# x's log decays made with features on partitions, summed by VectorE's prefix scans

## The chip, the cores and the metric

The kernel runs on one core of one Trainium2 chip. The metric is the device time of one execution in microseconds; lower is better. The engines are named as the profile names them: PE (TensorE's matmuls, with PEld for its weight loads), DVE (VectorE), ACT (ScalarE), POOL (GpSimd) and SP (SyncE, which here issues most of the loads).

## The reference

Two transformer blocks over 256 tokens of width 2048. The change lies in the second one, in its gated linear attention over x (4 heads, key width 128 each, so 512 key features; the 256 tokens are 2 chunks of 128; one gate runs forward, one backward):

```python
la = log_sigmoid(d @ wd2 + bd) / 16          # log decay, one per token and key feature, for each way
# per chunk and way:
b = cumsum(la, over tokens)                  # running sums
b_last = b[-1]                               # whole chunk
scores[i, j] = sum_d q[i,d] k[j,d] exp(b[i,d] - b[j,d])      (j <= i)
o = scores @ v + (q * exp(b)) @ s
s = exp(b_last) * s + (k * exp(b_last - b)).T @ v            # the state that the next chunk takes
```

The same is done for the 256 context tokens before, which only leave their state `s`. The rest of the block (the projections, a spatial gating, the output product and a feed-forward part) is matrix products with `w_in_2`, `w_out_2` and so on.

## The kernel before

Every large product is made from chunks of weights: SP loads a 128 x 2 x 512 piece of weights into one of 4 slots of `ring`, DVE forms from it the sums that a seven-product (Strassen-like) scheme needs (`step(n)`: lines 1098 and 1099 are `step_first`, 1107 and 1109 are `step_last`), and PE multiplies (`chunk`, line 636: 14 products of 128x256, 28 passes in the trace, since an f32 product is two passes). `step` for chunk m makes the sums of chunk m+2, into one of 3 slots of `sums`. When a group of four chunks is done, ACT copies its first product (`first_keep`, line 2008) and DVE gathers the seven into the result (lines 1131 to 1141).

Each engine has its own program in a fixed, hand-written order. The order of what is done beside the chunks of the projection of x is a table, `MIX_BESIDE`: to (group, chunk) belongs a list of items, and each engine, when it has done its own part for that chunk, goes through the items and does what it has to do for each. The items that matter here, for the groups 1 and 2 (the keys k were group 0, the queries q are group 1):

- `la`: PE makes the log decays' raw values (line 879), ACT takes Abs, Exp, Ln of them, DVE ends them (`la_end`, lines 1540 and 1542).
- `k_turn`, `k_place`, `q_turn`, `q_place`: a 128x1024 tile is transposed in two steps, DVE's 32x32 block transposes (line 1190), then 16 copies of blocks by ACT (`place_blocks`, line 2043 or 2045).
- `cum`: PE makes the running sums of la as products with a triangular matrix (line 942), ACT copies them from PSUM to `b_t`, which has features on partitions (line 2377).
- `rem`: PE makes the remaining decays (the sums of la behind each token) with two other triangular matrices (line 949), ACT takes their Exp into `qe` (line 2395).
- `kdec`: DVE multiplies `qe` with the keys (line 1687); `upd` later has PE multiply this with the values.
- `level`: the scores are made in 8 levels of halved blocks. For each, DVE takes differences of `b_t` (line 1608), ACT takes their Exp (line 2345, two instructions), DVE and POOL multiply them with queries and keys (lines 1623 and 2720), and PE, behind the chunk to which the item belongs, multiplies the two (line 977). In PE's program this waits for DVE's and POOL's results:

```python
elif item[0] == "level":
    pe.wait_ge(s["lv_q"], lv + 1)
    pe.wait_ge(s["lv_k"], lv + 1)
```

On ACT the two Exp of a level come ahead of the other items of the same chunk. On DVE a level's differences come ahead of `step_first`, its product comes behind that, then `step_last`, then the other items of the chunk.

## Time and profile before

| | |
|---|---|
| median of 3 runs | 2707.28 us (2707.27 to 2708.39) |
| the profiled execution's own time | 2707.41 us |
| its span, from first to last instruction | 2705.6 us |
| PE busy | 2693.7 us, 100% of the span |
| DVE busy | 2108.5 us, 78% |
| ACT busy | 861.7 us, 32% |
| POOL busy | 315.0 us, 12% |
| DMA | 571.88 MB, mean 211 GB/s |

The span is that of one execution, recorded on the chip. The 1.8 us between the span and the execution's own time lie ahead of the first and behind the last instruction. Matmuls overlap, so that PE busy means that it had work, not that it was at its peak.

### The profile page before, as it was taken

Reading aid. Unit: us, or ns where it says so; the run is one execution under the profiler, and the core shown is the slowest. Engines: PE = TensorE matmul, PEld = TensorE weight load, DVE = VectorE, ACT = ScalarE, POOL = GpSimd, SP = SyncE. Lnnn points to the kernel's source line nnn. Section 1 sums busy time; section 2 is a strip of 40 time slices with the busy share of each in tenths; the row PEclk is TensorE's granted clock in tenths of the full one; section 3 lists DMA queues with packets and bytes.
Section 4 is the critical chain, followed back from the end, with each engine's and each line's share of the span. In section 5 each row is a group of like instructions: output and inputs, shape, how many; then the busy total and the mean of one; then the engine's idle time right before and its main releaser. Section 6 shows DMA issues by size and latency. Waiting matters only on the chain.

```text
span 2705.6 us, 27692 instructions
## 1 busy us (share of the span) xinstructions
PE 2693.7 (100%) x9684; PEld 1725.2 (64%) x9684; DVE 2108.5 (78%) x3066; ACT 861.7 (32%) x1986; POOL 315.0 (12%) x500
## 2 busy tenths in 40 slices
PE   9999999999999999999999999999999999999998
PEld 8888888886444444444447888888444444444487
DVE  7988887987999999998887677886866667664444
ACT  2455655332453534530036442331321211111000
POOL 2112231000101111010101012100010010100000
PEclk9999999999999999999999999999999999999999
DMA  8888777677666667668775655554576676656554
GB/s 279 246 264 255 250 236 232 206 235 237 218 221 219 214 218 221 221 233 275 259 273 167 172 171 141 148 186 157 172 223 219 214 221 217 187 164 202 174 175 132
DMA packets 277660, 571.88 MB, mean 211 GB/s; under 512 B 26056, under 2 KB 27420, under 8 KB 277008
## 3 DMA queue, kind: packets, MB, share of 16 engines
q1 hardware_dynamic: 244384, 460.05, 54.3%
q0 software_dynamic: 32704, 109.73, 12.5%
q8 instruction: 76, 1.25, 0.2%
q14 instruction: 64, 0.52, 0.1%
q10 hardware_dynamic: 432, 0.34, 0.0%
HBM read 565.91 MB, written 4.11 MB: 211 GB/s over the span
## 4 chain that ended last, share of the span: by engine, by line
PE 77%; issue 20%; DVE 1%; POOL 1%; POOLq 1%; DMA 0%; DVEq 0%; ACT 0%; ACTq 0%
PE PS L651 44%; PE PS L636 30%; PE PS L665 0%; DMA ring<-in_w_branch_a 0%; PE PS L924 0%; PE PS L774 0%; PE PS L800 0%; PE PS L977 0%; PE PS L722 0%; POOLq L2583 0%; POOL mem L2584 0%; PE PS L779 0%; POOLq L2581 0%; POOL small L2711 0%; PE PS L696 0%
## 5 line engine op out<-in xcount | busy, mean ns | idle before, releaser
L1098 DVE TENSOR_TENSOR sums<-ring 128x512 f32<-128x512 f32 x429 | 299.8, 699 | 411.6 <-PE PS L651 260.3
L651 PE MATMUL PS<-sums,mem 128*128 128x512 f32 x1100 | 561.5, 592 | 0.0
L636 PE MATMUL PS<-ring,mem 128*128 128x256 f32 x1936 | 543.8, 380 | 0.1
L636 PE MATMUL PS<-sums,mem 128*128 128x256 f32 x1792 | 533.0, 379 | 0.0
L651 PE MATMUL PS<-ring,act_t 128*128 128x512 f32 x1056 | 511.0, 592 | 1.4 <-issue 1.0
L651 PE MATMUL PS<-ring,mem 128*128 128x512 f32 x880 | 438.6, 592 | 0.0
L636 PEld LDWEIGHTS PS<-ring,mem 128*128 128x128 f32 x1936 | 365.9, 190 | 52.1 <-issue 2.1
L651 PEld LDWEIGHTS PS<-sums,mem 128*128 128x128 f32 x1100 | 209.0, 190 | 263.1 <-issue 262.8
L636 PEld LDWEIGHTS PS<-sums,mem 128*128 128x128 f32 x1792 | 340.5, 190 | 46.3
L651 PEld LDWEIGHTS PS<-ring,act_t 128*128 128x128 f32 x1056 | 200.1, 190 | 251.2 <-issue 246.6
L2008 ACT COPY first_q<-PS 128x256 f32<-128x256 f32 (+1 forms) x73 | 32.5, 445 | 1010.5 <-PE PS L651 669.0
L2043 ACT COPY mem<-mem 32x256 f32<-32x256 f32 (+1 forms) x784 | 313.4, 400 | 123.2 <-DVE mem L1935 84.8
L1109 DVE TENSOR_TENSOR sums<-sums,ring 128x512 f32<-128x512 f32 x429 | 302.1, 704 | 14.9
L1231 DVE SCALAR_TENSOR_TENSOR mem<-mem,small 128x1024 f32<-128x1024 f32 x240 | 302.0, 1279 | 8.6 <-DMA mem<-in_w_mod 8.5
L1107 DVE TENSOR_TENSOR sums<-sums,ring 128x512 f32<-128x512 f32 x429 | 302.0, 704 | 0.0
L1099 DVE TENSOR_TENSOR ring<-ring 128x512 f32<-128x512 f32 x431 | 300.8, 698 | 0.0
L651 PEld LDWEIGHTS PS<-ring,mem 128*128 128x128 f32 x880 | 167.0, 190 | 209.6 <-issue 208.3
L2595 POOL DMA_DIRECT2D mem<-in_w_mod x192 | 103.8, 541 | 1438.9 <-DVE mem L1231 1241.3
L636 PE MATMUL PS<-ring,act_t 128*128 128x256 f32 x976 | 265.1, 379 | 0.0
L636 PEld LDWEIGHTS PS<-ring,act_t 128*128 128x128 f32 x976 | 184.7, 190 | 26.8 <-issue 1.4
L651 PE MATMUL PS<-sums,act_t 128*128 128x512 f32 x352 | 179.8, 592 | 0.1
L651 PEld LDWEIGHTS PS<-sums,act_t 128*128 128x128 f32 x352 | 66.8, 190 | 84.6 <-issue 84.6
(305 smaller groups left out, 1935.3 us busy)
## 6 DMA issues: line engine op xcount, KB each, us to landing
ring<-in_w_in SPq DMA_DIRECT2D x240, 512.0 KB, 4.1
mem<-in_w_mod POOLq DMA_DIRECT2D x192, 512.0 KB, 4.7
ring<-in_w_up SPq DMA_DIRECT2D x176, 512.0 KB, 4.4
ring<-in_w_ffn_in SPq DMA_DIRECT2D x176, 512.0 KB, 4.6
ring<-in_w_down SPq DMA_DIRECT2D x88, 512.0 KB, 4.9
ring<-in_w_ffn_out SPq DMA_DIRECT2D x88, 512.0 KB, 3.8
ring<-in_w_out SPq DMA_DIRECT2D x64, 512.0 KB, 3.8
ring<-in_w_branch_a SPq DMA_DIRECT2D x16, 512.0 KB, 4.3
```

The lines of the kernel that those rows point to most:

```text
L636: mm = pe.matmul(product(g, j), of(j, 2 * (c if part is None else part) + q), weights(j, n, q), start=lead and opens, stop=tail, skip_grou ...
L651: mm = pe.matmul(product(g, j), of(j, c), weight[j], start=lead, stop=tail, skip_group_check=True)
L1098: ve.tensor_tensor(one, b11, b12, ADD).then_inc(s["sums_ready"], 1)
L1099: ve.tensor_tensor(b12, b22, b12, ADD)
L1107: ve.tensor_tensor(two, one, b22, ADD).then_inc(s["sums_ready"], 1)
L1109: ve.tensor_tensor(three, two, b21, ADD).then_inc(s["sums_ready"], 1)
L1231: op = ve.scalar_tensor_tensor(acc[which], wm[:, h % 2, :], col, acc[which], MUL, ADD)
L2008: act.copy(to, product(g, Q1)).then_inc(s["first_kept"], 1)
L2043: act.copy(to, from_[:, :, 0:tiles, b_, :])
L2595: pool.dma_start(wm[:, h % 2], w_mod[:, kt, col:col + 2 * CN]).then_inc(wm_loaded[h % 2], 16)
```

## The change

PE now makes x's raw log decays transposed: the weights `wd2` are the stationary operand and the projected tokens `d_t` the moving one, so that the result has features on partitions and tokens along the row. This takes 16 products of 128 columns where there were 4 of 512 (both on 32 rows of the array each). The running sums are made by four prefix scans of DVE (`tensor_tensor_scan`) straight into `b_t`; a tile `go_on` that is 1 except for a 0 at each head's first token restarts the sum. PE's `cum` and `rem` products are gone. The remaining decays are Exp(whole - b) on ACT, eight instructions of 128x128, each with its own bias column; the result has features on partitions, so DVE multiplies it with the transposed keys `k_t`, transposes it in blocks, and ACT places the blocks with 16 copies into `k_tok` (`kdec_place`). POOL's next two loads of `w_mod` wait for `la_done` where they waited for `rem_done`. The table names in TURN0 only shift by one.

```diff
-                      (1, 3): [("gather", 1), ("cum",)], (2, 0): [("q_turn",), ("q_place",)], (2, 1): [("rem", 0), ("rem", 1)],
-                      (2, 2): [("level", 0, 0), ("kdec", 0), ("kdec", 1)],
+                      (1, 3): [("gather", 1)], (2, 0): [("q_turn",), ("q_place",), ("cum",)], (2, 1): [("rem",)],
+                      (2, 2): [("level", 0, 0), ("kdec",), ("kdec_place",)],
...
 (PE)        def log_decay(m):
                 pe.wait_ge(s["d_placed"], m + 1)
-                for h in range(2):
-                    for r in range(2):
-                        rows = slice(64 * h + 32 * r, 64 * h + 32 * r + 32)
+                quarters = [(h, r, slice(64 * h + 32 * r, 64 * h + 32 * r + 32)) for h in range(2) for r in range(2)]
+                if m == 0:
+                    for h, r, rows in quarters:
                         mm = pe.matmul(PS[:, 4 + 2 * h + r, :], d_t[rows, h * P:(h + 1) * P], wd2[rows, :], start=True,
                                        stop=True)
+                else:
+                    for hd in range(GH):
+                        for h, r, rows in quarters:
+                            mm = pe.matmul(PS[:, 4 + 2 * h + r, hd * P:(hd + 1) * P], wd2[rows, hd * P:(hd + 1) * P],
+                                           d_t[rows, h * P:(h + 1) * P], start=True, stop=True)
...
-                    elif item[0] == "cum":
-                        pe.wait_ge(s["la_ready"], 2)
-                        for n in range(2):
-                            for r in range(2):
-                                for hd in range(GH):
-                                    mm = pe.matmul(PS[:, 4 + 2 * n + r, hd * P:(hd + 1) * P],
-                                                   la[:, n, r, hd * P:(hd + 1) * P], tri[:, r, :], start=True,
-                                                   stop=True)
-                        mm.then_inc(s["cum_done"], 1)
-                    elif item[0] == "rem":
-                        r = item[1]
-                        pe.wait_ge(s["cum_kept"], 1)
-                        mm = pe.matmul(PS[:, 6 + r, :], tri[:, 2 + r, :], la[:, r, r, :], start=True, stop=True)
-                        mm.then_inc(s["rem_done"], 1)
                     elif item[0] == "upd":
                         r = item[1]
-                        pe.wait_ge(s["kdec_ready"], 3 + r)
+                        pe.wait_ge(s["kdec_placed"], 1)
...
 (DVE)
+                    elif item[0] == "cum":
+                        ve.wait_ge(s["state_done"], 2)
+                        ve.wait_ge(s["la_ready"], 2)
+                        ve.memset(go_on, 1.0)
+                        ve.drain()
+                        ve.memset(go_on[:, 0:CN:P], 0.0)
+                        ve.drain()
+                        for n in range(2):
+                            for r in range(2):
+                                way = slice(None, None, 1 - 2 * r)
+                                op = ve.tensor_tensor_scan(b_t[:, n, r, way], go_on, la[:, n, r, way], 0.0, MUL, ADD)
+                        op.then_inc(s["cum_kept"], 1)
...
                     elif item[0] == "kdec":
-                        r = item[1]
-                        ve.wait_ge(s["rem_exp"], 2 + r)
-                        ve.tensor_tensor(qe[:, r, :], qe[:, r, :], k_tok[:, r, :], ALU.mult)\
-                            .then_inc(s["kdec_ready"], 1)
-                        if r == 1:
-                            ve.memset(s_t[:], 0.0)
+                        ve.wait_ge(s["rem_exp"], 2)
+                        for r in range(2):
+                            part = qe[:, r, :].rearrange("p (h i) -> p h i", i=P)
+                            ve.tensor_tensor(part, part, k_t[:, :, r * P:(r + 1) * P], ALU.mult)
+                        flat = qe.rearrange("p r f -> p (r f)")
+                        turn_in_blocks(flat, flat)
+                        ve.memset(s_t[:], 0.0)
...
 (ACT)
-                    elif item[0] == "cum":
-                        act.wait_ge(s["cum_done"], 1)
-                        act.copy(b_t.rearrange("p a b c -> p (a b) c"), PS[:, 4:8, :]).then_inc(s["cum_kept"], 1)
...
                     elif item[0] == "rem":
-                        r = item[1]
-                        act.wait_ge(s["rem_done"], 2 + r)
-                        act.activation(qe[:, r, :], PS[:, 6 + r, :], ACT.Exp).then_inc(s["rem_exp"], 1)
+                        act.wait_ge(s["cum_kept"], 1)
+                        for r in range(2):
+                            edge = HD - 1 if r == 0 else 0
+                            for hd in range(GH):
+                                whole = b_t[:, r, r, hd * P + edge:hd * P + edge + 1]
+                                op = act.activation(qe[:, r, hd * P:(hd + 1) * P], b_t[:, r, r, hd * P:(hd + 1) * P],
+                                                    ACT.Exp, bias=whole, scale=-1.0)
+                        op.then_inc(s["rem_exp"], 1)
+                    elif item[0] == "kdec_place":
+                        turned(act, "kdec", 0)
+                        for a_ in range(4):
+                            for b_ in range(4):
+                                from_ = qe[32 * a_:32 * a_ + 32].rearrange("p r (h b c) -> p r h b c", b=4, c=32)
+                                to = k_tok[32 * b_:32 * b_ + 32].rearrange("p r (h d) -> p r h d", d=P)
+                                act.copy(to[:, :, :, 32 * a_:32 * a_ + 32], from_[:, :, :, b_, :])
+                        act.drain().then_inc(s["kdec_placed"], 1)
...
 (POOL)
-            pool.wait_ge(s["rem_done"], 3)
+            pool.wait_ge(s["la_done"], 2)
             mod_loads(2)
```

What stands in a row on ACT between the queries' placing (L2045) and the Exp of the levels 0 and 1 (L2345, the shapes 4x64 and 8x32), before:

```order
L2008 COPY first_q<-PS 128x256
L2377 COPY mem<-PS 128x2048
L2045 ACTIVATE mem<-mem 32x2x4x32 x16
L2395 ACT_TABLE_LOAD
L2395 ACTIVATE mem<-PS 128x512 x2
L2345 ACTIVATE mem<-mem 128x2x4x64 x2
L2345 ACTIVATE mem<-mem 128x2x8x32 x2
L2008 COPY first_q<-PS 128x256
```

The same place of ACT's program in the changed kernel, whose line numbers are 4 higher there:

```order
L2012 COPY first_q<-PS 128x256
L2049 ACTIVATE mem<-mem 32x2x4x32 x16
L2399 ACT_TABLE_LOAD
L2399 ACTIVATE mem<-mem 128x128 x8
L2349 ACTIVATE mem<-mem 128x2x4x64 x2
L2408 COPY mem<-mem 32x8x32 x16
L2349 ACTIVATE mem<-mem 128x2x8x32 x2
L2012 COPY first_q<-PS 128x256
```

The copy of the running sums is gone, the two Exp of 128x512 are eight of 128x128, and the 16 placing copies (L2408) stand between the Exp of level 0 and those of level 1.

On DVE, from the sums behind the queries' block transposes (L1190) to the differences of level 1 (the second L1608), before:

```order
L1190 STREAM_TRANSPOSE mem<-mem 128x1024
L1098 TENSOR_TENSOR sums<-ring 128x512
L1099 TENSOR_TENSOR ring<-ring 128x2x256
L1107 TENSOR_TENSOR sums<-sums,ring 128x512
L1109 TENSOR_TENSOR sums<-sums,ring 128x512
L1608 TENSOR_TENSOR mem<-mem 128x512 x2
...
L1687 TENSOR_TENSOR mem<-mem 128x512 x2
L1690 MEMSET mem 128x512
L1608 TENSOR_TENSOR mem<-mem 128x512 x2
```

And in the changed kernel, where these lines are 8 lower (4 higher behind the new item):

```order
L1182 STREAM_TRANSPOSE mem<-mem 128x1024
L1667 MEMSET mem 128x512
L1669 MEMSET mem 128x4
L1674 SCALAR_TENSOR_TENSOR mem<-mem 128x512 x4
L1090 TENSOR_TENSOR sums<-ring 128x512
...
L1691 TENSOR_TENSOR mem<-mem 128x512 x2
L1182 STREAM_TRANSPOSE mem<-mem 128x1024
L1694 MEMSET mem 128x512
L1600 TENSOR_TENSOR mem<-mem 128x512 x2
```

The four scans (listed as SCALAR_TENSOR_TENSOR) and two fills stand behind the queries' transposes, and another block transpose stands behind the two kdec products. On PE the 16 products of L942 and the two of L949 are gone.

## Rows read from the trace of the kernel before

**Rows 1.** The page: busy time of the engines, and the chain that ended last.

```profile
PE 2693.7 (100%) x9684; PEld 1725.2 (64%) x9684; DVE 2108.5 (78%) x3066; ACT 861.7 (32%) x1986; POOL 315.0 (12%) x500
...
PE 77%; issue 20%; DVE 1%; POOL 1%; POOLq 1%; DMA 0%; DVEq 0%; ACT 0%; ACTq 0%
```

**Rows 2.** The chain in order of time: start us, us, what.

```profile
1573.42 3.57 PE PS L942 x32
1576.99 12.09 PE PS L636 x56
1589.08 1.72 PE PS L949 x4
1590.80 6.04 PE PS L636 x28
1596.84 0.62 PE PS L977 x16
1597.45 6.24 PE PS L636 x28
1603.69 0.39 PE PS L977 x32
```

**Rows 3.** Timeline of PE: start us, us, engine, line, op, tiles, shapes, count.

```profile
1539.37 1.93 PE L862 MATMUL PS<-mem 128*32 128x256 f32 x32
...
1553.95 1.14 PE L879 MATMUL PS<-mem 32*128 32x512 f32 x8
```

**Rows 4.** Timeline of ACT, from the queries' placing to level 1.

```profile
1578.92 6.79 ACT L2045 ACTIVATE mem<-mem 32x256 f32<-32x256 f32 x16
1585.84 1.28 ACT L2395 ACT_TABLE_LOAD   x1
...
1591.45 1.15 ACT L2345 ACTIVATE mem<-mem 128x512 f32<-128x512 f32 x2
1598.57 1.15 ACT L2345 ACTIVATE mem<-mem 128x512 f32<-128x512 f32 x2 [5.97 <-DVE mem L1608]
```

**Rows 5.** Timeline of DVE, the same stretch.

```profile
1577.27 1.25 DVE L1190 STREAM_TRANSPOSE mem<-mem 128x1024 f32<-128x1024 f32 x1
1583.14 0.69 DVE L1098 TENSOR_TENSOR sums<-ring 128x512 f32<-128x512 f32 x1 [4.63 <-PE PS L636]
...
1592.73 1.36 DVE L1623 TENSOR_TENSOR mem<-mem 128x256 f32<-128x256 f32 x2 [2.26 <-ACT mem L2345]
...
1595.34 1.28 DVE L1687 TENSOR_TENSOR mem<-mem 128x512 f32<-128x512 f32 x2
1596.68 0.48 DVE L1690 MEMSET mem<- 128x512 f32 x1
...
1599.75 1.72 DVE L1623 TENSOR_TENSOR mem<-mem 128x256 f32<-128x256 f32 x2
```

**Rows 6.** Timeline of POOL, the keys of level 1.

```profile
1599.28 1.92 POOL L2720 TENSOR_TENSOR mem<-mem 128x256 f32<-128x256 f32 x2 [5.46 <-ACT mem L2345]
```

**Rows 7.** Timeline of ACT: a placing behind its transpose, and small activations with two column operands.

```profile
1534.18 6.61 ACT L2401 COPY act_t<-act_t 32x256 f32<-32x256 f32 x16 [5.78 <-DVE act_t L1678]
...
1899.98 0.81 ACT L2467 ACTIVATE act_t<-PS,small 128x128 f32<-128x128 f32 x2 [1.79 <-PE PS L1033]
```

**Rows 8.** The page's costliest groups: busy us, mean ns, idle before.

```profile
L1231 DVE SCALAR_TENSOR_TENSOR mem<-mem,small 128x1024 f32<-128x1024 f32 x240 | 302.0, 1279 | 8.6 <-DMA mem<-in_w_mod 8.5
```

**Rows 9.** Timeline of PE at the two ends of the span.

```profile
1.42 3.36 PE L722 MATMUL PS<-ones 128*128 128x128 f32 x14 [1.42 <-POOLq L2602]
4.57 1.06 PE L696 MATMUL PS<-ident,x_tok 128*128 128x128 f32 x4
...
8.02 0.60 PE L696 MATMUL PS<-ident,x_tok 128*128 128x128 f32 x4
...
2696.78 1.03 PE L602 MATMUL PS<-act_t,mem 128*128 128x256 f32 x4
```

**Rows 10.** Windows: engines' busy us (count), granted PE clock, DMA share, GB/s.

```profile
2700.00:2701.00 1.00, 0.00 (x0) 0.00 (x0) 1.00 (x1) 0.00 (x0) 0.00 (x0) 0.64 0.00 0
```

More of the change, by code:

```diff
@@ L257, in build @@
         la, b_t = cut(3072, 2, 2, CN), cut(0, 2, 2, CN)
-        e_buf, qe = cut(5120, 2, CN), cut(6144, 2, CN)
+        e_buf, qe, go_on = cut(5120, 2, CN), cut(6144, 2, CN), cut(6144, CN)
         mix2_tmp, mix2_junk = [cut(7168 + 1024 * n, 2, CN) for n in range(3)], cut(7168, D)
@@ L301, in build @@
             "attn_done", "attn_kept", "bias_loaded", "bias_used", "ws_stored", "ws_spread", "c_ready",
-            "consts_loaded", "ctx_loaded", "cum_done", "cum_kept", "d_copied", "d_done", "d_kept", "d_placed", "d_summed",
+            "consts_loaded", "ctx_loaded", "cum_kept", "d_copied", "d_done", "d_kept", "d_placed", "d_summed",
             "decay_ready", "down_added", "exps_done", "gain_loaded", "ident_loaded", "forms_ab", "forms_ctx", "forms_ffn",
             "forms_ffn2", "forms_h", "forms_h2", "forms_hx", "forms_m", "forms_mix", "forms_w2", "den_ready", "x_first", "w_first", "sums_first", "gates_squashed",
-            "g_opened", "gate_loaded", "gate_ready", "gate_stored", "hidden_done", "job_acc", "half_done", "kdec_ready", "kt_kept", "la_done", "la_exp", "la_ready",
+            "g_opened", "gate_loaded", "gate_ready", "gate_stored", "hidden_done", "job_acc", "half_done", "kdec_placed", "kdec_ready", "kt_kept", "la_done", "la_exp", "la_ready",
             "levels_loaded", "lv_diff", "lv_done", "lv_exp_k", "lv_exp_q", "lv_k", "lv_q", "lv_taken", "masks_loaded", "max_ready",
@@ L394, in build @@
         TURN0 = {"heads": 0, "probs": 7, "merged": 15, "ffn": 19, "up": 23, "ctx": 45, "mix2": 49, "ws": 53, "k": 54, "q": 55,
-                 "y0": 56, "u0": 57, "y1": 58, "u1": 59, "ffn2": 58, "up2": 62}
+                 "kdec": 56, "y0": 57, "u0": 58, "y1": 59, "u1": 60, "ffn2": 59,
+                 "up2": 63}
         PLACE0 = {"heads": 0, "probs": 7, "merged": 15, "ffn": 19, "ctx": 23, "mix2": 27, "ffn2": 29}
@@ L936, in _ @@
                         log_decay(1)
-                    elif item[0] == "cum":
-                        pe.wait_ge(s["la_ready"], 2)
-                        for n in range(2):
-                            for r in range(2):
-                                for hd in range(GH):
-                                    mm = pe.matmul(PS[:, 4 + 2 * n + r, hd * P:(hd + 1) * P],
-                                                   la[:, n, r, hd * P:(hd + 1) * P], tri[:, r, :], start=True,
-                                                   stop=True)
-                        mm.then_inc(s["cum_done"], 1)
-                    elif item[0] == "rem":
-                        r = item[1]
-                        pe.wait_ge(s["cum_kept"], 1)
-                        mm = pe.matmul(PS[:, 6 + r, :], tri[:, 2 + r, :], la[:, r, r, :], start=True, stop=True)
-                        mm.then_inc(s["rem_done"], 1)
                     elif item[0] == "upd":
                         r = item[1]
-                        pe.wait_ge(s["kdec_ready"], 3 + r)
+                        pe.wait_ge(s["kdec_placed"], 1)
                         kept_all(pe, G0["mix"] + VV_GROUP + 1)
                         if r == 0:
-                            pe.wait_ge(s["rem_exp"], 3)
+                            pe.wait_ge(s["cum_kept"], 1)
                         else:
@@ L960, in _ @@
                             mm = pe.matmul(PS[:, 6 + hd // 2, (hd % 2) * T:(hd % 2) * T + T],
-                                           qe[:, r, hd * P:(hd + 1) * P], vv[:, r, hd * T:(hd + 1) * T],
+                                           k_tok[:, r, hd * P:(hd + 1) * P], vv[:, r, hd * T:(hd + 1) * T],
                                            start=True, stop=True)
@@ L1616, in level_close @@
                 if lv == 0:
-                    ve.wait_ge(s["rem_done"], 3)
                     ve.wait_ge(s["q_kept"], 1)
```

## The prediction

> **What bounds the kernel now.** I read the page first: PE has work for all of the span, and 77% of the chain that ended last is PE's matmuls, with nearly all the rest as PE's own issue [rows 1]. So what is taken off PE comes off the time one for one, and a new wait of PE is added one for one. DVE is busy for 78% and ACT for 32%; their work is free only as long as PE never stands for it. So the second view is the chain in order of time around the change [rows 2]: three chunks of 6.04 us, with the running sums (3.57 us) and the remaining decays (1.72 us) between them, then level 0, one chunk, level 1, back to back. There is no wait in it. The third views are the timelines of ACT and DVE beside it [rows 4 to 6], to see how early the results arrive that PE asks for. For level 1, PE comes at 1603.69; DVE's product for it ended at 1599.75 + 1.72 = 1601.47 and POOL's at 1601.20. That is 2.2 us of slack, and the change touches exactly the engines that fill it.
>
> **The change, part by part.** The sum is made against the profiled execution, 2707.41 us (median of the runs 2707.28, so 0.1 us apart).
>
> PE, removed: L942 3.57 us and L949 1.72 us, together -5.29 us [rows 2].
>
> PE, changed: the four 32-row products of 512 columns (8 passes, from 1553.95 to the next row at 1555.02, 1.07 us) become 16 of 128 columns (32 passes). They stream the same columns. The old ones plainly ran four beside each other: 8 passes of 512 columns one behind the other would take 8 x 0.43 = 3.4 us (0.43 being a quarter of L949's 1.72 us for 4 passes). If the new ones do so too, the nearest row is L862, 32 passes of 256 columns on quarters of the array in 1.86 us (1539.37 to the next row at 1541.23) [rows 3]; half the columns gives 0.93 us at the least. If none runs beside another, it is L942's price, 3.57 us. I take 1.2 us, near the lower end, since the order in the code still goes round the four quarters: +0.13 us, with ends at -0.14 and +2.5.
>
> DVE, added behind the queries' transpose, which ends at 1578.52: a fill of 128x512 (0.48 us), a tiny one, two drains (0.2 us together with it) and four scans. The trace shows no scan. By half of the 128x1024 row of the same listed operation, 1.28 us, one takes 0.64 us [rows 8]; as the upper end I take that whole row. So they end between 1581.8 and 1584.3. The cover is DVE's idle time of 4.63 us before 1583.14 [rows 5] and then the two chunks by which `step` runs ahead of PE. ACT asks for `b_t` at 1586.8 (below); DVE must still make one chunk's sums (four rows from 1583.14 on, 2.6 us) and two differences (1.3 us) before 1589.4. So the scans cost nothing up to (1589.4 - 3.9 - 1579.2) / 4 = 1.57 us each, and 4 us per us beyond that.
>
> The Trainium skill ("DVE: opcode table, instruction layouts, handler registers and perf-mode slots", section 6, Datapath and trigger behaviour) says that the built-in scan feeds its result back and runs at half throughput. No row here shows one; by that rule a scan would be about 1.2 us, still inside the cover, where by the row's price it is 0.64, and the sum is the same by both. It brings the limit nearer, though, and speaks for the last rival below.
>
> ACT, up to level 0: the copy of the running sums (between the gather's `first_keep` and 1578.92) is gone, so the queries' placing starts as the transpose ends, at 1578.56 (a placing starts some 0.04 us behind it, as L2401 does behind its own) instead of 1578.92. It takes 6.79 us, then 0.13 us and the table load of 1.28 us [rows 4]: 1586.76. Eight Exp of 128x128 with a bias column follow. Nearest is L2467, the same size with two column operands: two take 0.81 at 0.45 each, so one each 0.36 us, and eight take 2.97 [rows 7]. The other end is a quarter of half of the 1.15 us that two of 128x512 take, 1.15 us for eight. I take 2.6, near the row of the same size: 1589.4. From the start of the level's Exp to the end of DVE's product it was 1594.09 - 1591.45 = 2.64 us [rows 4, 5], so level 0 is ready at 1592.05. PE, after 12.09 + 6.04 us of chunks from 1573.42, asks for it at 1591.55. **First wait: 0.5 us** where there was none.
>
> The Trainium skill ("ScalarE: Activation LUTs", section What ACT_TABLE_LOAD costs) puts an activation with one column operand at 280 ns + 0.833 ns an element, with 93 ns of overlap between neighbours. That is 0.29 us for each of 128 columns and 2.4 for eight, and an estimate of the whole sum 0.2 us below mine.
>
> ACT, level 1: this is the step on which the prediction rests. In ACT's program the 16 copies of `kdec_place` stand between the Exp of level 0 and those of level 1. They need DVE's transpose of the kdec product, and that stands behind level 0's product and `step_last`. From DVE's level-0 product to its kdec products it was 1595.34 - 1592.73 = 2.61 us, and 1.34 us to the row behind them [rows 5]. With level 0's Exp at 1589.4, DVE's product starts 1.28 later at 1590.7, kdec at 1593.3, the transpose at 1594.65, ending at 1595.9 (1.25 as L1190). ACT's 16 copies take 6.61 us [rows 7] and a drain 0.1: 1602.65. Only then do level 1's Exp run; before, from their start at 1598.57 DVE's product took until 1601.47, 2.90 us [rows 4, 5], and POOL's until 1601.20, 2.63 us [rows 4, 6]. Level 1 is ready at 1605.55. PE, from 1592.1 on, does level 0 (0.62) and a chunk (6.24) and asks at 1598.95. **Second wait: 6.6 us.** Queued behind it on PE is all that follows; DVE's `step_last` and gather stand behind its product of level 1, ACT's `first_keep` behind the Exp. PE's next level comes two chunks (12 us) later, which I take as enough for DVE to catch up.
>
> So PE starts level 1 at 1605.6 instead of 1603.69: +1.9 us, and +2.05 with the log decays. As a ledger: -5.29 + 0.13 + 0.5 + 6.65 = +2.0.
>
> The clock: at the start of the span PE, having done nothing, runs 14 passes of 128 columns in 3.36 us, 0.24 us each, where 32 such take 3.57 us in mid-kernel, 0.11 each; four transposes take 1.06 us at 4.57 and 0.60 at 8.02 [rows 2, 9]. So it ran at the lower level (1.2 GHz) from 1.42 until about 7.1. At the end, PE's last row ends at 2697.8, and in the window from 2700 to 2701 the granted clock is 0.64, on its way to half [rows 9, 10]. So it falls some 2.5 us behind the last matmul. A wait of 6.6 us is longer than that. If PE then needs the 5.7 us that it needed at the start, it does 2.85 us' less work than at 2.4 GHz: **+2.85 us**. The end of this term towards nothing is a clock that stays or that rises at once.
>
> DVE, ACT and DMA elsewhere: nothing. POOL's two loads of `w_mod` (512 KB each) go out 36 us earlier, at about 1555, beside SP's ring loads. DVE then stands for ACT's Abs, Exp and Ln anyway. DVE's extra transpose and the strided kdec operand are in the chain above.
>
> Sum: -5.29 + 0.13 + 0.5 + 6.6 + 2.85 = +4.8 to 4.9, so 2707.4 + 4.9 = **2712.3 us**. What a measurement of this kernel can tell from no change is about 0.2%, 5.4 us: this forecast lies just inside it.
>
> **The rivals.**
> 1. As summed, with both waits and the lower clock: 2712.3. Its own range: the eight Exp move level 1 by -1.45 to +0.4, the time at the lower clock may be half or a fifth more of that at the start (-1.4 to +0.6), the copies by 0.5 each way: 2709.8 to 2714. Chance 0.68.
> 2. The waits come, the clock does not fall (or is back at once): 2707.4 + 2.05 = 2709.5 us. Against it stands the fall 2.5 us behind the last matmul [rows 9, 10]. Chance 0.10.
> 3. Not slower: the placing is hidden and PE keeps the whole saving, -5.16, so 2702.3. One thing would do it: ACT's chain from the queries' transpose to level 1 being 7.1 us shorter than I make it (1605.55 against 1598.4), from which on nothing is lost; it is no slower from 2.05 us shorter on, if the clock holds in the 4.6 us of waiting that are left. For it speaks only that the price of the eight Exp is not in the trace; against it, 6.61 us of copies and 6.79 of placing are rows. Chance 0.08.
> 4. More than summed: the 32-row products no longer run beside each other (+2.4, 2714.7), or scans above 1.57 us each (at 2 us, +1.7, 2714.0), or DVE, which comes out of level 1 later against PE than before, makes PE wait once more at the next levels (of 1 to 3 us). Chance 0.14.
>
> **How the numbers follow.** The predicted time is that of the first. From 2709.0 to 2715.3 the range takes in the first, the second and most of the fourth, and leaves out the third (0.08) and the fourth's far part. Slower by over 0.2% means above 2712.7: the fourth nearly whole (0.13) and some 0.4 of the first (0.27), together 0.40. Faster by over 0.2%, below 2701.9, is a third of the third case: 0.03. Within: 0.57.
>
> **What would show it.** In the changed kernel: ACT's 16 copies between the Exp of levels 0 and 1, starting about 1596 and ending about 1602.6; PE idle before level 1 for 6 to 7 us and before level 0 for less than 1, with DVE's or POOL's level product as releaser; the granted clock below 1 in a window behind it, and passes of 256 columns at twice 0.216 us for some 5 us; four scans of 0.6 to 1.3 us ending before ACT's table load; the 32-row products in 1.0 to 1.3 us. It is wrong if PE shows no wait before level 1, or if waits of DVE's or PE's turn up elsewhere of the same size.

## The result: 4.4 us slower, and the profile after

The changed kernel takes 2712.16 us, the median of 20 runs (2710.95 to 2713.22); the kernel before, beside it, 2707.72 us (2706.71 to 2708.39). The ratio is 1.0016, 95% interval 1.0010 to 1.0022. PE lost the 18 products of the running sums and the remaining decays, and the kernel became 4.4 us slower, 0.16%. That is less than the 0.2% of the prediction's bound, but the interval leaves out 1, so the slowdown is told from none. The profiled execution took 2712.94 us, its span 2711.1 us, so 5.5 us more than before.

The page of the changed kernel, with the lines that answer to [rows 1]:

```profile
PE 2691.7 (99%) x9672; PEld 1723.3 (64%) x9672; DVE 2115.2 (78%) x3073; ACT 867.3 (32%) x2007; POOL 313.2 (12%) x500
...
PE 76%; issue 20%; DVE 2%; ACT 1%; POOL 1%; POOLq 1%; DMA 0%; DVEq 0%; ACTq 0%
```

PE has 2 us less work, though the clock stretched some of it, and its share of the chain is a point lower; DVE and ACT have come into the chain. Which line they came in by is told by the view of PE's waits, changed kernel (line, releaser: us in total, times, longest):

```profile
PE PS L969 <- DVE mem L1614: 7.2, 3, 6.2
...
PE PS L637 <- DVE mem L1123: 0.4, 1, 0.4
```

L969 is the level's product on PE (before L977) and L1614 DVE's product for it (before L1623). Before there was no such wait in this stretch. ACT's timeline of the changed kernel, to be held against [rows 4]:

```profile
1578.32 6.80 ACT L2049 ACTIVATE mem<-mem 32x256 f32<-32x256 f32 x16 [7.31 <-DVE mem L1182]
1585.25 1.28 ACT L2399 ACT_TABLE_LOAD   x1
1586.55 2.45 ACT L2399 ACTIVATE mem<-mem 128x128 f32<-128x128 f32 x8
1588.90 1.13 ACT L2349 ACTIVATE mem<-mem 128x512 f32<-128x512 f32 x2
1595.42 6.61 ACT L2408 COPY mem<-mem 32x256 f32<-32x256 f32 x16 [5.39 <-DVE mem L1182]
1602.13 1.15 ACT L2349 ACTIVATE mem<-mem 128x512 f32<-128x512 f32 x2
```

The 16 copies (L2408) take ACT from 1595.42 to 1602.03, and only then do level 1's Exp run, 3.6 us later than before. DVE in the same stretch, to be held against [rows 5]:

```profile
1577.04 1.25 DVE L1182 STREAM_TRANSPOSE mem<-mem 128x1024 f32<-128x1024 f32 x1
1578.35 0.48 DVE L1667 MEMSET mem<- 128x512 f32 x1
1579.08 4.57 DVE L1674 TENSOR_TENSOR_SCAN mem<-mem 128x512 f32<-128x512 f32 x4
...
1590.13 1.40 DVE L1614 TENSOR_TENSOR mem<-mem 128x256 f32<-128x256 f32 x2 [1.56 <-ACT mem L2349]
...
1592.78 1.29 DVE L1691 TENSOR_TENSOR mem<-mem 128x512 f32<-128x512 f32 x2
1594.14 1.25 DVE L1182 STREAM_TRANSPOSE mem<-mem 128x1024 f32<-128x1024 f32 x1
...
1603.31 1.39 DVE L1614 TENSOR_TENSOR mem<-mem 128x256 f32<-128x256 f32 x2 [4.80 <-ACT mem L2349]
...
1606.19 0.69 DVE L1123 TENSOR_TENSOR mem<-PS,first_q 128x512 f32<-128x512 f32 x1 [0.16 <-issue]
```

The scans end at 1583.65 (1579.08 + 4.57) and nobody waits for them. DVE stands 4.80 us for ACT's late Exp, and its gather (L1123) comes only at 1606.19. PE's timeline, to be held against [rows 2]:

```profile
1591.59 0.69 PE L969 MATMUL PS<-mem 128*64 128x64 f32 x16 [0.27 <-DVE mem L1614]
...
1604.76 0.66 PE L969 MATMUL PS<-mem 128*32 128x32 f32 x32 [6.24 <-DVE mem L1614]
1605.35 1.22 PE L637 MATMUL PS<-ring,mem 128*128 128x256 f32 x2
1606.94 1.22 PE L637 MATMUL PS<-ring,mem 128*128 128x256 f32 x2 [0.37 <-DVE mem L1123]
1607.95 1.06 PE L637 MATMUL PS<-sums,mem 128*128 128x256 f32 x2
...
1611.23 0.59 PE L637 MATMUL PS<-sums,mem 128*128 128x256 f32 x2
```

PE waits 6.24 us for level 1 and starts it at 1604.76, where it was 1603.62 by the same view (the chain in [rows 2] has 1603.69). Behind it a pair of 256-column passes takes 1.06 to 1.22 us, and 0.59 only from 1611.23 on: the clock. The windows of the changed kernel (length; busy us of PE, PEld, DVE, ACT, POOL; granted clock; DMA share; GB/s):

```profile
1598.00:1601.00 3.00, 0.52 (x3) 0.11 (x1) 0.51 (x1) 2.92 (x8) 0.00 (x0) 0.97 0.57 181
1601.00:1604.00 3.00, 0.00 (x0) 0.00 (x0) 0.69 (x2) 2.41 (x6) 1.17 (x2) 0.50 0.19 73
...
1606.00:1610.00 4.00, 3.63 (x9) 2.53 (x8) 3.56 (x7) 0.00 (x0) 0.00 (x0) 0.50 0.00 0
...
1611.00:1612.00 1.00, 1.00 (x6) 0.90 (x5) 0.91 (x2) 0.00 (x0) 0.00 (x0) 0.96 0.00 0
```

A mean of 0.97 in the first window is 0.17 us at half; 0.96 in the last is 0.08 us. So the clock was at the lower level from 1600.8 to 1611.1, 10.2 us. Of these 3.9 lie in the wait for level 1 and 0.4 in the gather's wait; the other 5.9 us had work and cost about 3.0 us. All 20 executions have a mean granted clock of 0.997 or 0.998, where 87 executions of the kernel before, taken beside the experiments, have 0.999 or 1.0; so the slow stretch is not a matter of the profiled one alone.

The ledger of the changed kernel, by the times of PE's timeline: level 1 starts 1.14 us later; from there to level 2 is 16.06 us where it was 12.68 (+3.4: the clock 3.0, the gather's wait 0.37). Level 6, at 1655.82, brings another wait of 0.64 us, and from there on the changed kernel is 5.24 us behind. The last 0.3 us of the span's 5.5 come at 1903, far behind this stretch, where PE's weight loads wait 0.27 us for POOL; what brought that about is not shown. Ahead of the change the changed kernel's profile is 0.26 us earlier (L863 at 1539.11, before L862 at 1539.37), so by its own doing level 1 is 1.4 us later.

The wait at 1655.82 is of another kind than the first ones. The levels 2 to 5 had none, so DVE had caught up. Then DVE stood for a load of the ring, the changed kernel first, then the kernel before:

```profile
1644.79 0.69 DVE L1090 TENSOR_TENSOR sums<-ring 128x512 f32<-128x512 f32 x1 [5.49 <-DMA ring<-in_w_in]
```

```profile
1637.71 0.69 DVE L1098 TENSOR_TENSOR sums<-ring 128x512 f32<-128x512 f32 x1 [2.37 <-DMA ring<-in_w_in]
```

From 1644.79 on DVE's rows follow each other without a gap of over 0.16 us up to level 6's product. Why this load came late is not shown.

### The profile page after: what moved, and what is told of

It reads as the page before. It is cut to its first block, busy times and chain, and to the rows that moved or that the text cites. A ratio compares the mean times of both kernels' runs of the same rounds, so it can differ in the third digit from the quotient of the medians.

```text
span 2711.1 us, 27701 instructions
## 1 busy us (share of the span) xinstructions
PE 2691.7 (99%) x9672; PEld 1723.3 (64%) x9672; DVE 2115.2 (78%) x3073; ACT 867.3 (32%) x2007; POOL 313.2 (12%) x500
## 4 chain that ended last, share of the span: by engine, by line
PE 76%; issue 20%; DVE 2%; ACT 1%; POOL 1%; POOLq 1%; DMA 0%; DVEq 0%; ACTq 0%
PE PS L652 44%; PE PS L637 29%; PE PS L666 0%; DMA ring<-in_w_in 0%; PE PS L930 0%; PE PS L801 0%; PE PS L775 0%; DVE mem L1614 0%; ACT mem L2049 0%; ACT mem L2408 0%; PE PS L723 0%; PE PS L806 0%; PE PS L780 0%; DVE sums L1099 0%; POOL small L2725 0%
```

## The experiments

The theory after the result was the prediction's first case. The saving on PE (5.2 us) is real; the copies of `kdec_place`, which nobody needs soon, stand on ACT ahead of level 1's Exp; PE waits for these, its clock falls, and both together cost more than the saving. The rivals: that DVE's own new work, not the copies, makes the wait; that the saving is not there; that the clock costs nothing; that the scans or the 32-row products cost more than they show.

| kernel | median us | runs | span us | ratio to before, 95% |
|---|---|---|---|---|
| the change | 2712.16 | 20 | 2711.1 | 1.0016 (1.0010 to 1.0022) |
| e3_kept_busy | 2710.57 | 11 | 2708.8 | 1.0014 (1.0005 to 1.0022) |
| e4_half_place | 2708.86 | 11 | 2707.4 | 1.0006 (0.9997 to 1.0015) |
| e9_quarter_place | 2707.34 | 11 | 2706.9 | 1.0000 (0.9991 to 1.0008) |
| e1_place_later | 2706.71 | 11 | 2704.0 | 0.9999 (0.9990 to 1.0008) |
| e2_all_behind | 2706.35 | 11 | 2704.7 | 0.9995 (0.9986 to 1.0004) |
| e6_gather_first | 2705.37 | 11 | 2703.5 | 0.9992 (0.9983 to 1.0001) |
| e7_scans_twice | 2710.64 | 10 | 2708.4 | 1.0013 (1.0004 to 1.0022) |
| e8_quarter_by_quarter | 2707.22 | 11 | 2705.4 | 0.9999 (0.9990 to 1.0008) |
| e11_wsum_later | 2703.92 | 11 | 2702.4 | 0.9988 (0.9980 to 0.9997) |
| e10_spread | 2702.64 | 11 | 2700.7 | 0.9983 (0.9974 to 0.9992) |

The kernel before took 2707.05 us beside e1 to e4, 2707.3 beside e6 to e9, 2707.07 beside e10 and e11.

### e1_place_later: the copies behind level 1's Exp

```diff
-                      (2, 2): [("level", 0, 0), ("kdec",), ("kdec_place",)],
-                      (2, 3): [("level", 0, 1), ("gather", 2)],
+                      (2, 2): [("level", 0, 0), ("kdec",)],
+                      (2, 3): [("level", 0, 1), ("gather", 2), ("kdec_place",)],
```

> The placing of kdec is moved behind level 1's Exp and first_keep on ACT; nothing else. Theory (the 16 copies ahead of level 1's Exp hold PE, and the clock falls in that wait): level 1's Exp then wait only for DVE's differences, which ended at 1596.01 + 1.29 = 1597.3 in the changed kernel's trace; with 2.5 to 2.9 us from there, level 1 is ready at 1600.0 where PE asks for it at 1598.5, so a wait of about 1.5 us stays instead of 6.2, too short for the fall 2.3 us behind the last matmul, so no clock term: 6.2 - 1.5 + 3.4 = 8.1 us less than the changed kernel, about 2704.1. Rival (it is DVE's extra transpose and the scans that make level 1 late, the copies only lie beside): the wait stays near 6 us and the time at 2712. Second rival (the lower clock comes with the change whatever PE waits): wait gone, time near 2707.

PE's rows with a wait, e1:

```profile
1600.22 0.46 PE L969 MATMUL PS<-mem 128*32 128x32 f32 x32 [1.77 <-DVE mem L1614]
...
1602.40 0.70 PE L637 MATMUL PS<-ring,mem 128*128 128x256 f32 x2 [1.09 <-DVE mem L1123]
```

Moving the copies alone takes 5.5 us off the time of the change (4.8 us when each is held against the kernel before beside it), so it was they that made the kernel slower than before. They are about half of the 9.6 us (4.4 + 5.2) between the change and a kernel that keeps its whole saving. It doesn't give the 2704.1: level 1 still waits 1.77 us, and PE now waits for DVE's gather, 1.09 and a further 0.17 us. DVE's rows show why, e1:

```profile
1592.71 1.28 DVE L1691 TENSOR_TENSOR mem<-mem 128x512 f32<-128x512 f32 x2
1594.08 1.25 DVE L1182 STREAM_TRANSPOSE mem<-mem 128x1024 f32<-128x1024 f32 x1
1595.38 0.48 DVE L1694 MEMSET mem<- 128x512 f32 x1
1595.94 1.29 DVE L1600 TENSOR_TENSOR mem<-mem 128x512 f32<-128x512 f32 x2
```

The kdec products, their transpose and the fill stand in front of level 1's differences (L1600), which therefore end at 1597.2; PE comes for the level at 1598.4. The rival "DVE's own new work" is a second, smaller cause that the copies had covered.

### e2_all_behind and e6_gather_first: first the kdec work behind the levels, then behind the gather too

The entries of the table that change:

```diff
-(2, 1): [("rem",)],
-(2, 2): [("level", 0, 0), ("kdec",), ("kdec_place",)],
-(2, 3): [("level", 0, 1), ("gather", 2)],
+(2, 2): [("level", 0, 0), ("rem",)],
+(2, 3): [("level", 0, 1), ("kdec",), ("gather", 2)], (3, 0): [("kdec_place",)],      # e2
+(2, 3): [("level", 0, 1), ("gather", 2), ("kdec",)], (3, 0): [("kdec_place",)],      # e6
```

> The remaining decays' Exp go behind level 0's Exp, the kdec products and their transpose behind level 1's product, the placing to the chunk after. Theory: both levels are then ready ahead of PE (level 0 at about 1590 against 1591.3, level 1 at about 1595.5 against 1598), PE has no wait and keeps the whole saving, 3.57 + 1.72 - 0.03 = 5.2 us under the kernel before: about 2702.4, 0.998 of it. Rival (the saving is given back later, since DVE's three added items are of 9 us and DVE makes PE wait at another place): between 2704 and 2708, with PE waits behind level 1.

> As the kernel with everything behind the levels, but on DVE the kdec products and their transpose stand behind the gather of group 2 and not ahead of it. Theory (what that kernel lost was PE's 2.05 us of waiting for the gather's first row and the lower clock behind it, 3.4 us at half level, 1.7 us): no wait of PE from the log decays to level 7, granted clock 1.0 throughout, and the whole saving of PE is kept, 3.57 + 1.72 - 0.03 = 5.2 us under the kernel before: about 2702. Rival (the saving is taken back by DVE's 9 us of added work wherever it is put): DVE makes PE wait for 2 us or more at level 2 or at a gather behind, and the time stays at 2705 to 2707.

In e2 the levels 0 and 1 cost PE nothing. The whole wait has gone to the gather, for which PE asks right behind level 1; e2:

```profile
1601.59 1.22 PE L637 MATMUL PS<-ring,mem 128*128 128x256 f32 x2 [2.05 <-DVE mem L1123]
```

The clock fell behind it for 3.4 us (pairs of passes at 1.22 us again). In e6 the gather of group 2 is in time, the clock stays at 1.0, and the waits have moved on to the levels 2 and 3 (and to the gather of group 3, 0.28 and 0.17 us), e6:

```profile
1612.02 0.46 PE L969 MATMUL PS<-mem 128*32 128x32 f32 x32 [1.34 <-DVE mem L1614]
1619.90 0.46 PE L969 MATMUL PS<-mem 128*32 128x32 f32 x32 [1.18 <-DVE mem L1614]
```

Level 2 waits because its Exp again stands behind the 16 copies (ACT, e6):

```profile
1602.60 6.61 ACT L2408 COPY mem<-mem 32x256 f32<-32x256 f32 x16 [6.77 <-DVE mem L1182]
1609.31 1.15 ACT L2349 ACTIVATE mem<-mem 128x512 f32<-128x512 f32 x2
```

Level 3 waits 1.18 us; in front of its differences DVE makes the spatial gating's sums (2.18 us), which e11 below moves. Both kernels fell short of the 2702 that was expected and lie, by their times, where their rivals had them. Each step brought something and uncovered the next item that stood ahead of something urgent.

### e4_half_place and e9_quarter_place: half and a quarter of the copies

```diff
-                        for a_ in range(4):
+                        for a_ in range(2):      # e4; range(1) in e9
```

> Only 8 of the 16 placing copies are made, at the same place, so half of k_tok is not the transposed product. Theory: level 1 is ready 3.3 us earlier, PE's wait is 2.9 us instead of 6.2. If the clock falls some 2.3 us behind the last matmul it falls in this wait too, and the whole is 3.3 us under the changed kernel, 2708.9; if the fall needs a longer wait, 3.3 + 3.0 = 6.3 us under it, 2705.9. Rival (copies not on PE's path): 2712.

> The changed kernel with 4 of the 16 placing copies, at the same place, so three quarters of k_tok are not the transposed product. Theory: level 1 is ready 4.97 us earlier than with 16, PE's wait is 1.27 us instead of 6.24, the gather's wait about 1.0 us; no fall of the clock, as in the kernel with waits of 1.8 and 1.1 us: 5.0 + 3.2 - 0.7 us under the changed kernel, about 2704.7. Rival (the fall needs no length of waiting, only a wait): 1.7 us more, 2706.4.

e4 leaves out 8 of the 16 copies and e9 leaves out 12, so that a part of `k_tok` is not what it should be. PE's rows with a wait, first e4:

```profile
1601.16 0.46 PE L969 MATMUL PS<-mem 128*32 128x32 f32 x32 [2.94 <-DVE mem L1614]
1603.33 1.22 PE L637 MATMUL PS<-ring,mem 128*128 128x256 f32 x2 [0.98 <-DVE mem L1123]
```

And e9:

```profile
1600.79 0.46 PE L969 MATMUL PS<-mem 128*32 128x32 f32 x32 [1.77 <-DVE mem L1614]
1602.96 1.22 PE L637 MATMUL PS<-ring,mem 128*128 128x256 f32 x2 [0.75 <-DVE mem L1123]
```

With 16, 8 and 4 copies level 1 waits 6.24, 2.94 and 1.77 us. The first 8 fewer take off 3.30 us, which is exactly 8 x 0.413 us (6.61 / 16). The next 4 take off 1.17 instead of 1.65 and end at the 1.77 of e1, which has none there: that is the floor that DVE's kdec work sets. The time of e4 was as expected, but not its path: the clock held through the wait of 2.94 us and fell 0.85 us after PE had resumed. The time of e9 is 2.6 us above what was expected. 0.5 us of it is the longer level wait; the gather's wait, 0.75 us, was in the forecast (about 1.0). The rest goes with its clock, which fell in the profiled execution (2708.70 us, one of the slower five of eleven; a window of e9, just behind the resumed work):

```profile
1602.00:1604.00 2.00, 1.25 (x4) 0.86 (x4) 1.66 (x4) 0.00 (x0) 0.00 (x0) 0.50 0.01 4
```

### e3_kept_busy: the wait stays, the clock doesn't fall

```diff
                     elif item[0] == "level":
+                        if lv == 1:
+                            turns_of_ones(26)
                         pe.wait_ge(s["lv_q"], lv + 1)
```

> The changed kernel with 26 products of ones (5.8 us at 2.4 GHz) put ahead of PE's wait for level 1; they leave the result alone. Theory: level 1 is ready at the same time as in the changed kernel (1604.7), the wait after the ones is some 0.4 us, the granted clock stays at 1.0, and what goes is the time at the lower clock: 3.4 us less the 0.4 us of the gather's wait, so 3.0 us under the changed kernel, about 2709.2. Rival (the 3.4 us between level 1 and level 2 are not the clock but the gather's and level 2's waits): no change from 2712.2.

PE, e3 (lines 2 higher than in the changed kernel from L969 on):

```profile
1598.61 5.97 PE L723 MATMUL PS<-ones 128*128 128x128 f32 x52
1605.03 0.46 PE L971 MATMUL PS<-mem 128*32 128x32 f32 x32 [0.45 <-DVE mem L1616]
...
1607.21 0.70 PE L637 MATMUL PS<-ring,mem 128*128 128x256 f32 x2 [1.09 <-DVE mem L1125]
```

A window of e3 shows the clock:

```profile
1604.00:1608.00 4.00, 2.45 (x44) 1.71 (x42) 3.62 (x7) 0.00 (x0) 0.70 (x1) 1.00 0.00 0
```

Useless products fill the wait, level 1 comes no earlier, and the kernel is faster by 1.6 us by the medians, or by 0.9 us when each is held against the kernel before beside it; the two ratios' intervals overlap, so it needs the profile to carry this reading. There PE takes 14.47 us from level 1 to level 2 (1605.03 to 1619.50) where it took 16.06 in the change: 1.59 us less. The profiled span is 2.3 us shorter, but what lies between 1.6 and 2.3 is not this stretch: 0.7 us are level 6, which does not wait here, and 0.3 the wait at 1903, less 0.26 by which the change's profile is earlier from the start. 3.0 us had been expected, near the whole price of the slow clock. But the slow clock had covered something: at full clock PE's next products come sooner, and the gather's wait is 1.09 and 0.17 us where it was 0.37. So the clock's net price was about 1.6 us.

### e7_scans_twice: the scans' price and their cover

```diff
-                        for n in range(2):
+                        for n in [0, 1, 0, 1]:
...
-                        op.then_inc(s["cum_kept"], 1)
+                            ve.drain()
+                        ve.drain().then_inc(s["cum_kept"], 1)
```

> The same, with the four scans made twice (the result is the same): 4.5 us more of DVE ahead of the sums and the differences, with some tenths for drains. Theory (the scans are covered by DVE's idle time and the lead of its sums, up to a limit): at 1.12 us each the one set is covered; with two sets the running sums are there 4.7 us later, level 0 is ready at about 1595.3 where PE asks at 1591.6, a wait of 3.7 us, and a fall of the clock behind it (1.7 to 3.4 us): 5.4 to 7.1 us over the kernel without, 2707.4 to 2709.1 if that one is at 2702. Rival (DVE has cover for all of it, being busy for only 78%): no difference. Rival (nothing of DVE is covered): the single set costs its 4.5 us too, and the kernel without is at 2706.

DVE, e7:

```profile
1578.46 9.58 DVE L1674 TENSOR_TENSOR_SCAN mem<-mem 128x512 f32<-128x512 f32 x8
```

And PE, e7:

```profile
1595.09 1.12 PE L969 MATMUL PS<-mem 128*64 128x64 f32 x16 [4.38 <-DVE mem L1614]
```

Eight scans take 9.58 us where four take 4.57; with the drains DVE is 5.3 us later than in e6, its parent. There DVE's product for level 0 ended at 1590.14 and PE came for it at 1591.09, so DVE had 0.95 us to spare, and 5.3 less 0.95 makes the 4.38 us that PE waits. The time is 5.27 us above e6 (5.4 to 7.1 had been expected): those 4.4, a fall of the clock behind them (3.4 us at half), less 0.6 us at level 2, which waits 0.72 instead of 1.34. DVE's chain is what level 0 comes after there, since `rem` is behind level 0. In the change the spare is larger: level 0's differences ended at 1587.4 and ACT, busy with the eight Exp, took them up only at 1588.90, 1.5 us later.

### e8_quarter_by_quarter: the order of the 32-row products

```diff
-                    for hd in range(GH):
-                        for h, r, rows in quarters:
+                    for h, r, rows in quarters:
+                        for hd in range(GH):
```

> The same as the first of this call, with the 16 products of the log decays in another order: all four heads of one quarter of the rows, then the next quarter. Theory (they run beside each other only when neighbours in the program are on different quarters of the array): they take up to 3.6 us instead of 1.1, and the time is 2.5 us over the kernel without, unless PE's shorter lead hides nothing. Rival (PE sets them beside each other in any order): no difference.

PE, e8:

```profile
1553.59 2.82 PE L885 MATMUL PS<-mem 32*128 32x128 f32 x32
```

And e6, its parent, in which they go round the four quarters as in the change:

```profile
1553.52 1.17 PE L885 MATMUL PS<-mem 32*128 32x128 f32 x32
```

The same 32 passes take 1.65 us more when neighbours in the program stand on the same quarter of the array, and the kernel 1.85 us, less than the 2.5 us that had been expected. In the change they do run beside each other (1.17 us).

### e11_wsum_later and e10_spread: nothing ahead of a level

e11 is e6 with `wsum_take`, an item of the spatial gating, moved behind the levels 2 to 4:

```diff
-                      (3, 1): [("level", 0, 2), ("wsum_take",)], (3, 2): [("level", 0, 3)],
-                      (3, 3): [("level", 0, 4), ("gather", 3)], (4, 0): [("upd", 0)],
+                      (3, 1): [("level", 0, 2)], (3, 2): [("level", 0, 3)],
+                      (3, 3): [("level", 0, 4), ("gather", 3)], (4, 0): [("upd", 0), ("wsum_take",)],
```

e10 also puts kdec in its place and the copies in three parts, each behind a level's Exp (`kdec_place` takes the range of its outer loop):

```diff
-                      (2, 3): [("level", 0, 1), ("gather", 2), ("kdec",)], (3, 0): [("kdec_place",)],
-                      (3, 1): [("level", 0, 2), ("wsum_take",)], (3, 2): [("level", 0, 3)],
-                      (3, 3): [("level", 0, 4), ("gather", 3)], (4, 0): [("upd", 0)],
+                      (2, 3): [("level", 0, 1), ("gather", 2)],
+                      (3, 1): [("level", 0, 2), ("kdec",), ("kdec_place", 0, 1)], (3, 2): [("level", 0, 3), ("kdec_place", 1, 2)],
+                      (3, 3): [("level", 0, 4), ("gather", 3), ("kdec_place", 2, 4)], (4, 0): [("upd", 0), ("wsum_take",)],
```

> From the kernel with the gather first, with only the spatial gating's sums (2.18 us of DVE) moved behind the gather of group 3. Theory: the wait at level 2 stays (1.34 us, ACT's copies), the wait at level 3 (1.18 us) and the gather's (0.45 us) go: 1.6 us under that kernel, about 2703.8. Rival (level 3 waits for ACT or for POOL, not for those sums): no change, 2705.4.

> From the kernel with the gather first: its trace shows PE waiting 1.34 us at level 2 (level 2's Exp on ACT stand behind the 16 placing copies once more, 1602.60 to 1609.2), 1.18 us at level 3 (DVE's 2.18 us of sums for the spatial gating in front) and 0.45 us at the next gather. Here the kdec products and transpose stand behind level 2, the copies in four parts between the levels' Exp (4, 4 and 8), and the spatial gating's sums one chunk behind the gather of group 3. Theory (each of the three waits is a queue of something that is not urgent in front of something that is; the work itself has room): all three waits go, 3.0 us under that kernel, about 2702.4, 4.9 us or 0.18% under the kernel before. Rival (DVE is the second bound of this stretch, so that the same waits come back a chunk later): 2704 to 2705.5.

e11 takes away level 3's wait and the gather's and leaves level 2's 1.34 us: 2703.92, as expected, though level 6 now waits 0.65 us (in e6 it had no wait). e10 takes level 2's wait too. ACT, e10:

```profile
1611.52 1.65 ACT L2408 COPY mem<-mem 32x256 f32<-32x256 f32 x4 [6.52 <-DVE mem L1182]
1613.43 1.15 ACT L2349 ACTIVATE mem<-mem 128x512 f32<-128x512 f32 x2 [0.27 <-DVE mem L1600]
1614.61 1.65 ACT L2408 COPY mem<-mem 32x256 f32<-32x256 f32 x4
...
1621.63 3.30 ACT L2408 COPY mem<-mem 32x256 f32<-32x256 f32 x8
```

PE's waits behind the log decays, e10:

```profile
PE PS L969 <- DVE mem L1614: 0.5, 1, 0.5
...
PE PS L637 <- DVE mem L1129: 0.2, 1, 0.2
```

The same work, the same instructions, 2702.64 us: 4.4 us under the kernel before (ratio 0.9983, 0.9974 to 0.9992) and 9.5 us under the change by the medians (8.9 when each is held against the kernel before beside it). By the profile level 1 starts 5.83 us earlier than before (1597.79 against 1603.62). Of this 0.58 us are there ahead of the change (L863 at 1538.79), so 5.25 are saved. The two waits that are left (the gather's 0.17 us and level 6's 0.45, with what PE loses as it starts again) give back 0.95: 4.3, near the median's 4.4. The span is 4.9 us shorter because it holds the 0.58 too.

## Why the prediction was right

It said 2712.3 us by its first case, slower through the copies on ACT and the clock; it is 2712.16. That was +4.9 us on an execution of 2707.41; the medians side by side differ by 4.4 us, and the kernel before stands 0.3 us higher beside it. Its steps one by one:

- **PE, removed (-5.29).** Right: in e10 PE stands 5.25 us earlier at level 1, which is 5.29 less the 0.04 of the log decays, and the kernel is 4.4 us under the one before.
- **Log decays (+0.13, 1.2 us for the 32 passes).** Right: 1.11 us (1553.69 to 1554.80), so +0.04. That they might not run beside each other was the fourth case's +2.4; with four neighbours on one quarter, in e8, it is 1.65 us.
- **Scans.** Under cover, as said, but the price from the nearest row, 0.64 us, was half of what they take: 1.20 us each, 4.57 for the four. The Trainium skill's page "DVE: opcode table, instruction layouts, handler registers and perf-mode slots" (section 6) states half throughput for the built-in scan, from which the prediction's estimate was about 1.2 us; the trace agrees. The limit of 1.57 us each was right: 4 x (1.57 - 1.2) makes 1.5 us of spare, and the differences lay 1.5 us before ACT took them up. That what goes beyond the cover comes through one for one, e7 shows (5.3 us more of DVE, 0.95 us of cover in its parent, 4.38 us of wait).
- **Eight Exp (2.6).** 2.45 us, nearer to the 2.4 that the prediction estimated from the Trainium skill's page "ScalarE: Activation LUTs" (section What ACT_TABLE_LOAD costs) than to the row of [rows 7].
- **First wait (0.5).** 0.27 us. ACT reached its placing 0.24 us earlier than I made it, since the whole trace is earlier there.
- **Second wait (6.6).** 6.24 us, with the copies at 6.61 as summed. They began at 1595.42 instead of 1595.9. Level 1 started 1.14 us later, or 1.40 after the 0.26 us between the profiles, instead of 2.05. Shown to be the copies by e1, e4 and e9.
- **The clock (+2.85).** Gross about 3.0 us (5.9 us of work at the lower level, where 5.7 were summed); net of what it covered, about 1.6 (e3), since the sum did not ask what a slow PE hides. Both of its times were read from one execution. In the twelve profiles the clock rises between 4.3 (e7) and 7.5 us (e2) from the start of the span, where the sum took 7.1, and falls 2.5 (before) to 4.8 us (e9) behind the last matmul, where it took 2.5. A wait of 6.6 us is longer than all of these, so the fall was safe to forecast; that its price came so close is in part luck.
- **"PE's next level comes two chunks (12 us) later, which I take as enough for DVE to catch up."** For the levels this held: the next four do not wait. But it left out the gather, which I had named as queued behind DVE's product. PE asks for it right behind level 1, and DVE came 0.37 us late; at full clock it is 1.26 (e3).
- **"DVE, ACT and DMA elsewhere: nothing."** This failed by 0.7 us: the load of the ring that DVE stood 5.49 us for, and behind it the wait at level 6. Another 0.3 us came at 1903.

So the forecast came within 0.2 us by errors that cancel in part: it put level 1 0.65 us later than it came, and it missed the gather, level 6 and the last 0.3 us (1.4 together). By the profile the loss is 5.5 us, by the medians 4.4, and the +4.9 lies between them; the profiled execution, 2712.94 us, is 0.8 above the median. What the forecast had right is the order of things on ACT and their price; the last half microsecond is luck.

The range of the first case, 2709.8 to 2714, is narrower at its low end than its own parts: -1.45, -1.4 and -0.5 make 2709.0. Nothing hangs on it, since the whole range began at 2709.0.

The third case, that PE keeps its saving if ACT's chain were 7.1 us shorter, was too simple as well: e1 takes the 6.61 us away and gets 2706.7, not near 2702.3, because DVE's own kdec work and the gather then hold PE.

## What to carry to other kernels

Work on the busiest engine that stands between two of another engine's due times is also their cover: taking 5.2 us off PE made everything behind it due 5.2 us sooner, and each item that nobody needed soon (copies, kdec, a spatial gating's sums) turned into a wait where it stood in front of one that was. So when such work is removed, list what every other engine does before each thing that the engine asks for next, the gather as much as the level, and move what is not urgent behind it, in pieces small enough to fit. That made +4.4 us into -4.4 us here. Remove a wait and look for the next at once, since a lone wait often covers a second one, and a slow clock a third.

## What the hardware showed that I had not expected

- **The clock fell after short waits, and not always.** In e9 PE waited 1.77 us, went on, and the granted clock was at half behind it, from 1601.4 for 6.8 us; in e1, with the same 1.77 us, it stayed at 1.0 in the profiled execution. There and in e9 the gather's wait followed (1.09 and 0.75 us). In e4 it fell at 1602.0, 0.85 us after PE had resumed from 2.94 us. The stretches at the lower level were about 10.2 us (the change), 6.8 (e4, e9) and 3.4 (e2, e7). From the start of PE's wait to the fall it was 2.0 us in e2, 2.3 in the change, 2.4 in e9, 3.8 in e4 and 4.2 in e7. So a wait of 2.05 us was enough in e2, and PE had gone on working before the fall in e4 and e9; what decides in a single case is not shown.
- **The runs of one kernel scatter, in part with the clock.** e6 and e10, whose clock did not fall, lie within 0.4 and 0.8 us. e9's eleven runs are spread from 2705.65 to 2708.81, e1's from 2705.78 to 2708.87. The record has the mean granted clock of each: it is 0.998 in e9's five slowest (from 2708.16 on), in e4's six slowest (from 2708.86 on), in e7's two slowest and in e1's slowest, and 0.999 or 1.0 in all others of these kernels. So in these the slower executions are those with more time at the lower level. e2's are four at 2704.5 to 2704.8 and seven at 2706.0 to 2706.8, which lies near the 1.7 us that 3.4 us at half cost; three digits of the mean are too few to see that, so for e2 it stays open. The clock is not all of it: e3 (2710.11 to 2711.78) and the kernel before (2706.60 to 2708.98 beside e6 to e9) scatter too, at 0.999 or 1.0 throughout. e1's profile is that of its fastest execution, so its span is 1.6 us under that of before, and its median only 0.3.
- **How far small products on quarters of the array run beside each other depends on their order:** 32 passes of 128 columns took 1.17 us where the program goes round the quarters (e6), and 2.82 with four neighbouring products on one quarter (e8).
- **A prefix scan of 128x512 takes 1.20 us,** about twice the 0.64 us that half of the 128x1024 row of [rows 8] would make it.
